# A hybrid decoder step on one core: the group norm by feature tile, layer norms with fused sums, expert ranks ahead of the weights

## The reference

```python
# _rwkv7, end: y (tokens x 8 heads x 64) out of the state recurrence
mu = y.mean(-1, keepdims=True)
var = jnp.square(y - mu).mean(-1, keepdims=True)
y = ((y - mu) * lax.rsqrt(var + RW_GN_EPS)).reshape(b, s, RW_WIDTH) * rw_gn_g + rw_gn_b
y = (y + bonus.reshape(b, s, RW_WIDTH)) * g
# _layer
merged = sigmoid(g_sb) * (o_sb @ w_sb_o) + sigmoid(g_mem) * (o_mem @ w_mem_o) + sigmoid(g_rw) * (o_rw @ w_rw_o)
h = _layer_norm(DN_ALPHA * x + merged @ w_out, ln1_g, ln1_b)
y = _layer_norm(DN_ALPHA * h + _moe(h, ...), ln2_g, ln2_b)
# _layer_norm
mu = xf.mean(-1, keepdims=True); var = jnp.square(xf - mu).mean(-1, keepdims=True)
return (xf - mu) * lax.rsqrt(var + LN_EPS) * g + b
# _moe: logits = h @ w_router + b_router, top 4 of 32 experts, softmax over the 4,
# each token's rows through its experts' (1024 -> 2048 -> 1024) clamped SwiGLU, weighted sum
```

## Time and profile before

| | us |
|---|---|
| median of three runs (1714.25 to 1716.26) | 1716.01 |
| the profiled execution, its own time | 1706.75 |
| its span | 1705.0 |
| PE busy (share) | 1527.2 (90%) |
| DVE busy | 595.3 (35%) |
| ACT busy | 279.8 (16%) |
| POOL busy | 149.3 (9%) |
| mean granted TensorE clock | 0.944 |

### The profile page before, as it was taken

One profiled execution on the slowest core, in us unless ns is written; L12 is line 12 of the kernel. 1 busy time (PEld: TensorE's weight loads), 2 busy tenths in 40 slices (PEclk: granted clock), 3 DMA queues, 4 the chain that ended last, 5 costly groups with the idle time before them and its releaser, 6 DMA issues.

```text
span 1705.0 us, 20920 instructions
## 1 busy us (share of the span) xinstructions
PE 1527.2 (90%) x7762; PEld 810.9 (48%) x7762; DVE 595.3 (35%) x904; ACT 279.8 (16%) x538; POOL 149.3 (9%) x271
## 2 busy tenths in 40 slices
PE   7977867778899997789999999999999999999993
PEld 5856523455698874443434343434333333433331
DVE  1689633156734545421212121212112121212125
ACT  1100233113322111211111101110111011111102
POOL 5422142102011001000000000000000000000000
PEclk9989988788989988889999999999999999999997
DMA  8689797766311105449999999999999999999990
GB/s 310 228 318 331 241 322 266 275 230 186 124 26 50 50 1 198 194 171 420 429 428 429 429 428 429 429 428 429 429 428 429 429 428 428 429 429 428 429 419 26
DMA packets 83913, 534.10 MB, mean 313 GB/s; under 512 B 8640, under 2 KB 9723, under 8 KB 59283
## 3 DMA queue, kind: packets, MB, share of 16 engines
q1 hardware_dynamic: 69714, 487.61, 69.9%
q0 software_dynamic: 14144, 45.79, 8.1%
HBM read 528.91 MB, written 4.46 MB: 313 GB/s over the span
## 4 chain that ended last, share of the span: by engine, by line
PE 58%; DMA 28%; DVE 7%; issue 4%; ACT 2%; POOL 1%; POOLq 0%; SPq 0%; DVEq 0%; ACTq 0%
PE bank L728 56%; DMA projT<-in_w_gate_up 24%; PE bank L729 2%; DMA ring<-in_w_in 2%; DVE ring L1639 1%; DMA ring<-in_cache_sb_k 1%; DMA ring<-in_w_mem_kv 1%; DVE ring L1728 1%; DVE sample_logits L1645 1%; DVE arena L1730 1%; ACT arena L1386 0%; DVE arena L2103 0%; POOLq L452 0%; POOL arena L610 0%; ACT L1427 0%
## 5 line engine op out<-in xcount | busy, mean ns | idle before, releaser
L728 PE MATMUL bank<-arena 128*128 128x128 f32 (+9 forms) x2172 | 335.3, 358 | 23.3 <-DVE arena L1681 8.7
L728 PEld LDWEIGHTS bank<-arena 128*128 128x128 f32 (+4 forms) x2172 | 230.2, 182 | 134.2 <-issue 123.2
L728 PE MATMUL bank<-ring,memT 128*64 128x512 f32 (+2 forms) x1152 | 282.8, 599 | 8.7 <-ACT memT L1585 7.6
L728 PE MATMUL bank<-projT,ring 128*128 128x264 f32 x1056 | 262.4, 406 | 29.8 <-DMA ring<-in_w_in 20.9
L2043 DVE TENSOR_SCALAR arena<-bank 128x256 f32<-128x256 f32 x64 | 26.9, 421 | 637.6 <-PE bank L728 637.6
L728 PEld LDWEIGHTS bank<-projT,ring 128*128 128x128 f32 x1056 | 207.3, 200 | 76.5 <-issue 20.6
L728 PE MATMUL bank<-projT 128*64 128x512 f32 (+1 forms) x1056 | 235.2, 591 | 8.6 <-DMA projT<-in_w_gate_up 8.6
L728 PE MATMUL bank<-ring,projT 128*64 128x512 f32 x1024 | 230.3, 597 | 0.0
L728 PEld LDWEIGHTS bank<-ring,memT 128*64 128x64 f32 (+2 forms) x1152 | 85.2, 139 | 156.6 <-issue 138.5
L728 PEld LDWEIGHTS bank<-projT 128*64 128x64 f32 (+1 forms) x1056 | 76.9, 141 | 161.8 <-issue 136.2
L728 PEld LDWEIGHTS bank<-ring,projT 128*64 128x64 f32 x1024 | 69.3, 137 | 147.4 <-issue 147.4
(11 more groups left out here) (272 smaller groups left out, 935.5 us busy)
## 6 DMA issues: line engine op xcount, KB each, us to landing
ring<-in_w_gate_up SPq DMA_DIRECT2D x64, 2048.0 KB, 21.2
projT<-in_w_gate_up SPq DMA_DIRECT2D x64, 2048.0 KB, 23.8
ring<-in_w_down SPq DMA_DIRECT2D x64, 2048.0 KB, 20.4
ring<-in_w_in SPq DMA_DIRECT2D x13, 2048.0 KB, 8.8
ring<-in_cache_sb_k SPq DMA_DIRECT2D x64, 256.0 KB, 5.2
ring<-in_cache_sb_k POOLq DMA_DIRECT2D x64, 256.0 KB, 5.9
ring<-in_cache_sb_v SPq DMA_DIRECT2D x64, 256.0 KB, 5.1
ring<-in_cache_sb_v POOLq DMA_DIRECT2D x64, 256.0 KB, 5.4
```

What stands on the lines that cost most here:

```text
L728: mm = lambda out, l, r, first, last, **k: pe.matmul(out, l, r, start=first, stop=last, **k)
```

## The change

Four edits in one. First, the group norm goes by feature tile: means and variances of tiles 0 and 1 are formed on PE inside the fourth chain part (after levels 1 and 3), DVE centres them after its level 1 and norms them before it waits for Z, and ACT takes their square roots after the X move of level 3. Tiles 2 and 3 follow after the part as before. Second, the output products of the RWKV branch start with those halves that need only tiles 0 and 1, in four banks instead of two (6, 0, 3, 7 in turn). Third, both layer norms take the row sum from the instruction that writes the residual (`accum_out`), and (x - mean) * gain is formed in `centred` while ACT works on the deviation; one instruction then scales it and adds the bias. Fourth, PE forms the ranks as soon as the choice of experts stands, beside the softmax weights on DVE; the counts get a group of their own ("count", bank 4) and stand behind the first gather.

```diff
...
     for dt in range(KT):
-        add(("o", 2, dt), 6 + dt % 2)
+        add(("o", 2, dt), (6, 0, 3, 7)[dt % 4])
...
-            g.wait_ge(sem("rw_done"), 1)
+            g.wait_ge(sem("rw_tile"), 4)
...
+            def group_mean(t):
+                for hp in range(2):
+                    gone(pe, ("ys", hp))
+                gone(pe, ("Y", 1, t // 2))
+                b = start(("gm", t))
+                done(("gm", t), mm(b[:, 0:T], blk64[:], T1[:, t, :], True, True))
+            def group_variance(t):
+                pe.wait_ge(sem("y_sq"), t + 1)
+                b = start(("gv", t))
+                done(("gv", t), mm(b[:, 0:T], blk64[:], T2[:, t, :], True, True))
...
+                    if it == 3 and lv == 1:
+                        group_mean(0)
+                        group_mean(1)
+                    elif it == 3 and lv == 3:
+                        group_variance(0)
+                        group_variance(1)
...
-            gone(pe, ("ys", 0))
-            gone(pe, ("ys", 1))
-            gone(pe, ("Y", 1, 0))
-            gone(pe, ("Y", 1, 1))
-            for t in range(4):
-                b = start(("gm", t))
-                done(("gm", t), mm(b[:, 0:T], blk64[:], T1[:, t, :], True, True))
-            over_heads("gv", T2, "y_sq", blk64)
-            branches(248, 256)
+            branches(248, 252)
+            group_mean(2)
+            group_mean(3)
+            branches(252, 256)
+            group_variance(2)
+            group_variance(3)
             arrived(pe, ("wo", 2))
             w = slot(("wo", 2)).rearrange("p (k n) -> p k n", k=4)
-            pe.wait_ge(sem("rw_done"), 1)
-            for dt in range(KT):
-                b = start(("o", 2, dt))
-                for k in range(4):
+            def rw_rows(dt, ks):
+                b = start(("o", 2, dt)) if ks[0] == 0 else bank[G.where[("o", 2, dt)][0]]
+                for k in ks:
                     last = mm(b[:, 0:T], w[:, k, dt * P:dt * P + P], pT[:, RW0 + k, :], k == 0, k == 3)
-                done(("o", 2, dt), last)
+                if ks[-1] == 3:
+                    done(("o", 2, dt), last)
+            pe.wait_ge(sem("rw_tile"), 2)
+            for dt in range(4):
+                rw_rows(dt, (0, 1))
+            pe.wait_ge(sem("rw_tile"), 4)
+            for dt in range(4):
+                rw_rows(dt, (2, 3))
+            for dt in range(4, KT):
+                rw_rows(dt, (0, 1, 2, 3))
...
+            pe.wait_ge(sem("weights_ready"), 1)
             for tt, (t0, rows) in enumerate(TOK):
                 last = tr(bank[7][0:NE, t0:t0 + rows], wt[0:rows, tt, 0:NE], rows)
             last.then_inc(sem("onewT_full"), 1)
             gather(0)
+            b = start("count")
+            for tt, (t0, rows) in enumerate(TOK):
+                last = mm(b[:, 0:NE], ones[0:rows, :], sel[0:rows, tt, 0:NE], tt == 0, tt == 2)
+            done("count", last)
             pe.wait_ge(free[rank_bank], opened[rank_bank])
+            gone(pe, "count")
             pe.wait_ge(sem("bias_in2"), 80)
             with pe.Fori(0, NE // 2) as p:
...
+            def deviations(tiles):
+                for t in tiles:
+                    move(("gv", t), T2[:, t, :], lambda b: b[:, 0:T], ACT.Sqrt, bias=eps[:, 0:1])
...
+                    if it == 3 and lv == 3:
+                        deviations((0, 1))
...
+            def centre(t):
+                b = take(v, ("gm", t))
+                tt_(T1[:, t, :], T1[:, t, :], b[:, 0:T], ALU.subtract).then_inc(freed_by(("gm", t)), 1)
+                gone(v, ("gm", t))
+                tt_(T2[:, t, :], T1[:, t, :], T1[:, t, :], ALU.mult).then_inc(sem("y_sq"), 1)
+            def normed(tiles):
+                for t in tiles:
+                    gone(v, ("gv", t))
+                    ins = v.reciprocal(T2[:, t, :], T2[:, t, :])
+                link(ins)
+                for t in tiles:
+                    ins = stt(T1[:, t, :], T1[:, t, :], col(GNG + t), T2[:, t, :], ALU.mult, ALU.mult)
+                link(ins)
+                for t in tiles:
+                    ins = stt(T1[:, t, :], T1[:, t, :], col(GNB + t), BON[:, t, :], ALU.add, ALU.add)
+                link(ins)
+                for t in tiles:
+                    tt_(R[:, t, :], T1[:, t, :], GG[:, t, :], ALU.mult).then_inc(sem("rw_tile"), 1)
             first_blocks(0)
...
+                    if it == 3 and lv == 1:
+                        centre(0)
+                        centre(1)
+                if it == 3:
+                    normed((0, 1))
                 gone(v, ("Z",) + n)
...
-            def norm_mean(x, tt):
-                rows = TOK[tt][1]
-                s = lambda j: st_[0:rows, 8 * tt + j:8 * tt + j + 1]
-                link(v.reduce_sum(s(0), x[0:rows, tt, :], AX.X))
-                ts(s(3), s(0), -1.0 / D, None, ALU.mult).then_inc(sem("mean"), 1)
+            stat_of = lambda tt, j: st_[0:TOK[tt][1], 8 * tt + j:8 * tt + j + 1]
+            def norm_mean(tt, halves):
+                if halves == 2:
+                    ts(stat_of(tt, 3), stat_of(tt, 0), stat_of(tt, 5), -1.0 / D, ALU.add, ALU.mult).then_inc(sem("mean"), 1)
+                else:
+                    ts(stat_of(tt, 3), stat_of(tt, 0), -1.0 / D, None, ALU.mult).then_inc(sem("mean"), 1)
             def norm_apply(x, tt, i, g_, b_, ready):
                 rows = TOK[tt][1]
-                xr_ = x[0:rows, tt, :]
-                s = lambda j: st_[0:rows, 8 * tt + j:8 * tt + j + 1]
+                xr_, u = x[0:rows, tt, :], centred[0:rows, :]
+                s = lambda j: stat_of(tt, j)
                 dst = xr_ if i >= 3 else h1[0:rows, tt, :].rearrange("r (k p) -> r p k", k=KT)
                 shape = (lambda a: a) if i >= 3 else (lambda a: a.rearrange("r (p k) -> r p k", k=KT))
                 v.wait_ge(sem("mean"), i + 1)
+                if i % 3:
+                    v.wait_ge(sem(ready), i % 3)
+                stt(u, xr_, s(3), g_[0:rows, :], ALU.add, ALU.mult)
                 v.wait_ge(sem("deviation"), i + 1)
                 link(v.reciprocal(s(4), s(2)))
-                link(ts(xr_, xr_, s(3), s(4), ALU.add, ALU.mult))
-                link(tt_(xr_, xr_, g_[0:rows, :], ALU.mult))
-                tt_(dst, shape(xr_), shape(b_[0:rows, :]), ALU.add).then_inc(sem(ready), 1)
+                stt(dst, shape(u), s(4), shape(b_[0:rows, :]), ALU.mult, ALU.add).then_inc(sem(ready), 1)
...
-                        stt(xres[0:rows, tt, c], xres[0:rows, tt, c], ALPHA, b[0:rows, :], ALU.mult, ALU.add
-                            ).then_inc(freed_by(("res", tt, half)), 1)
+                        stt(xres[0:rows, tt, c], xres[0:rows, tt, c], ALPHA, b[0:rows, :], ALU.mult, ALU.add,
+                            accum_out=stat_of(tt, (0, 5)[half])).then_inc(freed_by(("res", tt, half)), 1)
                     for half in range(2):
                         gone(v, ("res", tt, half))
...
             link(tt_(S_, S_, W_, ALU.add))
+            v.sem_inc(sem("sel_ready"), 1)
             v.wait_ge(sem("exp_logits"), 1)
             link(tt_(E, E, S_, ALU.mult))
             link(v.reduce_sum(stat(3), E, AX.X))
             link(v.reciprocal(stat(4), stat(3)))
             link(tt_(W_, E, each(stat(4)), ALU.mult))
-            v.sem_inc(sem("sel_ready"), 1)
+            v.sem_inc(sem("weights_ready"), 1)
...
                 link(stt(natural(yacc[0:rows, tt, :]), h1[0:rows, tt, :].rearrange("r (k p) -> r p k", k=KT), ALPHA,
-                         natural(yacc[0:rows, tt, :]), ALU.mult, ALU.add))
-                norm_mean(yacc, tt)
+                         natural(yacc[0:rows, tt, :]), ALU.mult, ALU.add, accum_out=stat_of(tt, 0)))
+                norm_mean(tt, 1)
```

54 lines of the change are left out of this document (22 added, 32 removed).

## The result

The changed kernel takes 1696.12 us at the median (four runs, 1693.0 to 1699.25), the kernel before 1715.13 on the same chip (four runs, 1714.1 to 1716.26): a ratio of 0.9901, 95% interval 0.9877 to 0.9925, so 13 to 21 us faster. Forecast were 1697.3.

A forecast was written before the change was run, and what follows sets the result against it. The weight stream at full DMA rate bounds the loop and starts only after PE's loop entry. Gains 8.2 + 2.6 + 2.1 + 5.8 = 18.7 from 1716.01 give 1697.3 us, range 1693 to 1702 (8 in 10: 1690 to 1706).

The forecast's parts named there:

- Tiles 0 and 1 inside the part: Fourth chain part: extra PE products and DVE passes end the chain 4.9 us later, least 2.05, most some 7.
- The 0.4 for the TX add: Fourth chain part: added products and the mask product make DVE's TX add some 0.4 us late.
- The 2.4 on the chain at Z: Ahead of Z: 6.1 us of new DVE work meets 3.7 free, so 2.4 us stand on the chain.
- Tiles 2 and 3: Behind the fourth part: turned state to output products falls from 20.9 to about 13.8 us; last tile ready 2.2 earlier.
- the first rival: Fourth part: PE's 3 us wait for U brings the low clock, `merged` gains only 4; 1702 us, chance 0.14.
- `merged`: End of the output products: 2.2 + 6.0 = 8.2 us earlier, bounds 5 and 10.
- Two microseconds from the weights beside it cost nothing: Ahead of the first layer norm: x and its small follower may land as late as 676, so ln_in isn't late.
- Layer norms: First norm's last tile gains 2.6 us; second norm gains 5.8, bounds 4 and 6.3.
- Ranks: Before the loop: ranks first saves 2.6 us, counts behind the gather cost 0.5, net 2.1.
- The clock did not stay up from 716 to 740: Rival, before the loop: full clock shrinks PE's 18.09 us, some 8 on the chain; 1689 us, chance 0.10.
- The loop follows PE's entry: Opposing rival: the weight stream alone sets the end, only the second norm's 5.8 us remains; 1710 us, chance 0.05.
- PE did not fall to the lower clock in level 2: Rival, fourth part: PE falls to 1.2 GHz in level 2 until the group norm; 1720 us, chance 0.03.

The follow-up runs named there:

- n_late: The changed kernel with DVE norming tiles 0 and 1 after the fourth chain part instead of ahead of Z; 1692.52 us, 0.9896 of the kernel before.
- x_early: The changed kernel with POOL's loads of x, gains and biases issued ahead of their old place; 1694.55 us, 0.9889 of the kernel before.
- g_again: Second profile of the kernel before with only the group norm by tile and split output products; this execution took 1706.13 us.
- warm: The changed kernel with seven unused PE products, four ahead of the last logits and three behind; 1690.27 us, 0.9857 of the kernel before.
- r_only: The kernel before with the ranks edit alone; 1711.62 us, 0.9983 of the kernel before.

## Why the prediction was right, step by step

The time was right (1697.3, measured 1696.12), and every part has the forecast sign, but two of its steps were wrong and the sum of the pieces is 3.1 short. That the medians agree to 1.2 us is luck: the ratio gives 17.0 and the profile 15.6 where 18.7 was forecast, and the start alone scatters by up to 15.

**Tiles 0 and 1 inside the part.** Forecast: U 4.9 late; measured 4.13. Four products moved the last XT add by 1.72, some 0.445 each, where I took 0.51 by dividing a row's 2.05. That row holds the run-out of its last product too: four such instructions have 1.05 in the timeline, and the next row starts 0.89 behind their start. The 0.4 for the TX add left no trace at the last XT add, and it does not follow from its own terms: 1.9 of DVE work and a mask of 0.7 against 1.42 + 1.03 make 0.15 at most. The 2.4 on the chain at Z was right (2.41, by n_late).

**Tiles 2 and 3.** From the state's turn to the last pass I forecast 13.8, measured 13.2. But the turn came 6.24 late and not 4.9: PE's 12.10 from U to the turn instead of 9.99. That is the first rival's mechanism at half its price, 2.1 of 4: the state steps, 4.13 late, ran at 1.2 GHz throughout. I had looked at the clock only for the rival's case and left it out of the sum. `merged` gained 7.19 instead of 8.2.

**"Two microseconds from the weights beside it cost nothing".** This step failed. I took the 8.8 of the large x for its small follower too, and counted 2 us for the weights; the follower landed 14.8 after its issue, at 677.9 when the scatter of stage one is taken off, where 676 was the last moment by my own working. Because `merged` moved forward by 7.2 and POOL's loads by 1.4, SP's first load stood 3.5 behind it and no longer 9.3. x_early showed the fix (33.23), g_again the price where the layer norm is slow (6.86), and warm another execution of the same code in which x was in time (33.22). This fits that the group norm part alone gives nothing in the timed runs, with early loads 6.5, and that the three parts together (0.9901) give more than the sum of their single ratios, 0.9938.

**Layer norms.** 2.6 forecast and 2.95 measured; 5.8 and 6.08. The read-outs were a little too dear, 0.1 each forecast and 0.07 to 0.09 measured, and in the first norm I took them off on top of the wait for ACT: the mean stood at 712.73 and ACT began at 713.13, so they cost nothing there. The Trainium skill's statement (Vector Engine (DVE) Microarchitecture Reference, Points that are easy to get wrong) that such an instruction with two wide SBUF sources runs at half throughput did not hold here: 1.28 us, where the two-tensor product of the same size takes 1.23. My working of that rule was wrong as well: at 2.2 us each the six instructions would have lost some 3 us on what they replace, but the three sums saved (3.75) were left out, so the second norm would have stayed about even.

**Ranks.** 2.6 less and 0.5 given back forecast; 2.84 and 0.47 measured, in r_only 2.62 and 0.53. The forecast of 2.1 lies within the 1.6 to 2.9 that the profiles allow.

**The other rivals.** The clock did not stay up from 716 to 740 (0.57): warm, which brought the clock back for the gather only, gained 3.3, and what full clock throughout would give, 8 by my estimate, no run shows. The loop follows PE's entry: 928.22 and 928.49. PE did not fall to the lower clock in level 2 (1.00 from 610 to 626, 0.96 to 640).

**The marks that I named.** With the 8.12 of scatter taken off, the last pass ends at 655.55 (forecast 654.8), the w_out products start at 667.67 (667), the loop at 734.50 (731.5), and SP's first load in it at 739.2 (736). The loop's entry is under the 736 that I called wrong, and 3.0 over the forecast: 1.0 from A-B and 2.7 from the late load, less 0.6 of small gains. DVE did wait for ln_in past 676, which I had named as a sign against me.

**Still open.** The pieces give 15.6, the ratio 17.0, the medians 19.0. Start differs by up to 15 us between executions of the same instructions; between this kernel's profiles the first differences stand between 200 and 290 us, in the cache pages of stage one. Four runs a side don't average that away, so the differences may be chance; the runs can't show it. What makes stage one scatter was not tried.

## What to carry to other kernels

When work on the chain moves forward, look up for each load that it needs whether its issue moves too, and take the landing time of that load, not of a bigger one beside it; the row of the small one was missing from my argument. Price a new wait of TensorE with the instructions behind it at the lower clock: here 0.94 of waiting cost 2.7, and 2.4 cost 3.4 in one profile and 5.4 in three. Take more than one profile of the version that decides: one code had two patterns here. And cut profiles at instructions that both kernels share before comparing spans, for the scatter ahead of the change was as large as the change.

## What the runs showed of the chip that I had not expected

- A load of 32 KB on POOL's queue landed 5.0 to 14.8 us after its issue, the 1 MB load issued 0.7 ahead of it 5.3 to 9.9. With the first of three loads of 2 MB issued 3.5 behind the small one it took 14.0 to 14.8, with 5.2 or more between them 8.7 to 9.8.
- Reading an accumulated sum costs VectorE 0.07 to 0.09 us, and the accumulation adds nothing to its instruction.
- With 5.47 us of products that nobody needs ahead of it, the granted clock was back at 2.4 GHz for the 48-instruction gather, which took 5.62 instead of 7.93; with 3.76 us of them it took 8.40. That is one profile of each.
- Executions of the same instructions up to the fourth chain part differed by up to 15 us, and the granted clock fell 27.8 to 31.2 us behind that point.
